# Values in front of seven tables, their rounding some units later, and the output product in front of the low parts

## The reference

```python
def dilated_branch(q, k, v, pos, slopes, window, dil):
    s = einsum(q, keys of the band) * Dh ** -0.5
    s = s - slopes[head] * dist                  # linear in the distance, one slope a head
    s = where(|rel| <= half, s, NEG_INF)
    m = max(s); p = exp(s - m); l = sum(p)
    return (p @ v) / l, m + log(l)

def dilated_attention(q, k, v, pos, slopes):     # (window, dilation): (128, 1), (512, 4), (2048, 16)
    wts = softmax of the three log-denominators
    return sum(wts * the three outputs)

def neighbourhood_attention(q, k, v, rpb):       # a window of 8 rows by 16 columns of a grid, bias from a table
    return softmax(q k^T * d ** -0.5 + bias) @ v
```

## Time and profile before

| what | value |
| --- | --- |
| median of three runs | 4428.1 us |
| the profiled execution's own time | 4431.9 us |
| its span | 4430.1 us |
| TensorE matmul busy | 3857.9 us, 87% |
| VectorE busy | 2207.0 us, 50% |
| ScalarE busy | 1520.0 us, 34% |
| GpSimd busy | 1658.4 us, 37% |
| TensorE in the chain of work that ended last | 69% of the span |
| mean granted TensorE clock | 0.944 |

### The profile page before, as it was taken

The page is one execution under the profiler, slowest core; times in us unless marked ns, Lnnn a source line. Parts: engine busy times, 40 slices in busy tenths (PEclk is TensorE's granted clock), DMA queues, the critical chain, the costliest instruction groups (busy, mean ns, idle before and its releaser), DMA issues.

```text
span 4430.1 us, 53389 instructions
## 1 busy us (share of the span) xinstructions
PE 3857.9 (87%) x19336; PEld 3229.6 (73%) x19336; DVE 2207.0 (50%) x3799; ACT 1520.0 (34%) x2745; POOL 1658.4 (37%) x1380
## 2 busy tenths in 40 slices
PE   2999666788869798996999999689798996999998
PEld 1788555676768587875888888677687875888887
DVE  2444388651266476754454443466576743233333
ACT  2212143652233375652212212233575622222221
POOL 2523023643155361003544444355440015444442
PEclk9999888899979899998999999899899998999999
DMA  7666430733035542221223331135523121111111
GB/s 161 183 187 183 115 94 8 152 93 115 24 103 133 158 110 51 58 82 44 95 86 105 81 105 34 72 98 138 150 62 79 41 81 57 48 49 47 58 39 53
DMA packets 283998, 402.37 MB, mean 91 GB/s; under 512 B 43572, under 2 KB 205492, under 8 KB 283188
## 3 DMA queue, kind: packets, MB, share of 16 engines
q1 hardware_dynamic: 276824, 373.79, 30.3%
q10 hardware_dynamic: 6912, 25.17, 2.0%
HBM read 311.60 MB, written 96.45 MB: 92 GB/s over the span
## 4 chain that ended last, share of the span: by engine, by line
PE 69%; issue 8%; DVE 8%; POOL 5%; DVEq 3%; ACT 3%; SPq 2%; DMA 2%; POOLq 1%; ACTq 0%
PE ps L477 6%; PE ps L479 6%; PE ps L478 6%; PE ps L2218 5%; PE ps L2220 5%; PE ps L2219 5%; PE ps L2234 5%; PE ps L2236 5%; PE ps L2235 5%; PE ps L1720 2%; POOL rs L803 2%; PE ps L1411 2%; PE ps L1412 2%; PE ps L1421 1%; DVEq L1228 1%
## 5 line engine op out<-in xcount | busy, mean ns | idle before, releaser
L426 POOL TENSOR_TENSOR WL<-RAW,WH 128x1024 fp32r<-128x1024 f32 x226 | 556.5, 2476 | 702.1 <-ACT WH L408 691.9
L477 PE MATMUL ps<-WH,XTh 128*128 128x512 f32 (+1 forms) x1536 | 618.9, 403 | 74.3 <-issue 36.6
L479 PE MATMUL ps<-WL,XTh 128*128 128x512 f32 (+1 forms) x1536 | 606.4, 395 | 0.0
L478 PE MATMUL ps<-WH,XTl 128*128 128x512 f32 (+1 forms) x1536 | 605.8, 394 | 0.0
L408 ACT ACTIVATE WH<-RAW 128x1024 fp32r<-128x1024 f32 x226 | 233.6, 1057 | 794.9 <-PE ps L2236 347.4
L2254 DVE TENSOR_TENSOR X<-ps,X 128x512 f32<-128x512 f32 x512 | 349.1, 689 | 253.9 <-PE ps L2236 253.0
L2234 PE MATMUL ps<-WH,Hh 128*128 128x512 f32 x1024 | 401.3, 392 | 4.2 <-DVE X L2254 3.1
L2218 PE MATMUL ps<-XTh,WH 128*128 128x512 f32 x1024 | 400.1, 391 | 1.2 <-issue 1.2
L2219 PE MATMUL ps<-XTl,WH 128*128 128x512 f32 x1024 | 398.8, 389 | 0.0
L2220 PE MATMUL ps<-XTh,WL 128*128 128x512 f32 x1024 | 398.8, 389 | 0.0
L2236 PE MATMUL ps<-WL,Hh 128*128 128x512 f32 x1024 | 398.6, 389 | 0.0
(11 more groups left out here) (260 smaller groups left out, 7949.9 us busy)
## 6 DMA issues: line engine op xcount, KB each, us to landing
RAW<-w_all SPq DMA_DIRECT2D x232, 512.0 KB, 3.7
WM<-w_mod ACTq DMA_DIRECT2D x48, 512.0 KB, 4.3
WM<-w_mod SPq DMA_DIRECT2D x48, 512.0 KB, 3.9
X<-x SPq DMA_DIRECT2D x2, 4096.0 KB, 13.7
X_d<-X SPq DMA_DIRECT2D x2, 4096.0 KB, 13.9
QSd<-QA_d SPq DMA_DIRECT2D x16, 512.0 KB, 3.7
KHd<-KA_d SPq DMA_DIRECT2D x32, 256.0 KB, 5.6
KLd<-KA_d SPq DMA_DIRECT2D x32, 256.0 KB, 6.2
```

The costliest lines, as they stand in the source:

```text
L426: e.tensor_tensor(w_low(n), w_raw(n), w_high(n).bitcast(F32), ALU.subtract).then_inc(w_ready, 1)
L477: e.matmul(bank, a, w, start=(kc == 0), stop=False)
L478: e.matmul(bank, b, w, start=False, stop=False)
L479: j = e.matmul(bank, a, l, start=False, stop=(kc == K - 1))
```

## The change

It is one diff with three parts. SyncE in the dilated stage issues table 0 alone, then V and VFS of the first two heads, then tables 1 to 3, then the load of head 1, then tables 4 to 7. `value_high(0)` on ScalarE moves behind the exponential of unit 2, and `value_low(0)` on GpSimd in front of unit 3's bias (neighbourhood) or unit 2's table update (dilated). And VectorE does the output of a group ahead of the low parts of the same step instead of behind them. The helpers `band_act` and `band_dve` are shared by the neighbourhood and the dilated stage, so the second and third parts are in both; the latent attention has its own.

```diff
--- before.py
+++ after.py
@@ -1509,7 +1509,6 @@
                 e.activation(a.VHL[:, h % 2, :, 0:64], a.VS[:, h // 2 % 2, :, o0:o0 + 64], ACT.Copy)
                 e.drain().then_inc(s["vhi"], 1)
 
-            value_high(0)
             exps(0)
             for u in range(N_UNITS + 6):
                 if 1 <= u <= N_UNITS:
@@ -1518,6 +1517,8 @@
                     exps(u + 1)
                 if u % 4 == 0 and u >= 8:
                     copy_out(u // 4 - 2)
+                if u == 1:
+                    value_high(0)
                 if u % T == 5 and u + 3 < N_UNITS:
                     value_high(u // T + 1)
 
@@ -1582,10 +1583,10 @@
             for u in range(N_UNITS + 10):
                 if u + 1 < N_UNITS:
                     maxes(u + 1)
+                if u % 4 == 1 and u >= 13:
+                    output(u // 4 - 3)
                 if 1 <= u <= N_UNITS:
                     low(u - 1)
-                if u % 4 == 1 and u >= 13:
-                    output(u // 4 - 3)
 
         def value_low(e, a, h):
             s = a.s
@@ -1600,9 +1601,10 @@
 
         def na_pool(who, a):
             e, s = who.e, a.s
-            value_low(e, a, 0)
             for u in range(N_UNITS):
                 h, t = divmod(u, T)
+                if u == 3:
+                    value_low(e, a, 0)
                 if t == 0:
                     e.wait_ge(*a.loaded(h))
                 if u >= 3:
@@ -1630,6 +1631,8 @@
                     e.drain()
                     e.tensor_scalar(LM[:], LM[:], 2.0, None, ALU.mult)
                     e.drain()
+                if u == 2:
+                    value_low(e, a, 0)
                 e.wait_ge(s["max"], a.u0 + u + 1)
                 if g == 0:
                     parts = [(slice(c, 576, 4), slice(128, 272)), (slice(576, DIL_KEYS), slice(272, 384))]
@@ -1679,9 +1682,7 @@
                         e.dma_start(NAB[64 * a2:64 * a2 + 64, slot, :].rearrange("p (a b) -> p a b", b=GRID_W),
                                     NAB_d[h][:, 1 - a2:1 - a2 + NA_E, GRID_W - 1:2 * GRID_W - 1]).then_inc(ld, 16)
                 if a.kind == "dil" and h == 0:
-                    for k in range(3):
-                        for t in range(ND_FIRST[k], ND_FIRST[k + 1]):
-                            e.dma_start(ND[:, t, :], ND_d[t]).then_inc(s[f"nd{k}"], 16)
+                    e.dma_start(ND[:, 0, :], ND_d[0]).then_inc(s["nd0"], 16)
                 if h % 2 == 0:
                     vld = a.v_loaded(p)[0]
                     if p >= 2:
@@ -1695,6 +1696,9 @@
                         if p >= 2:
                             e.wait_ge(s["out"], a.g0 + 4 * p - 4)
                         load_v(e, ZB_d, p, p % 2, ZSn, vld)
+                if a.kind == "dil" and h < 2:
+                    for t in range(ND_FIRST[h + 1], ND_FIRST[h + 2]):
+                        e.dma_start(ND[:, t, :], ND_d[t]).then_inc((s["nd1"], s["nd2"])[h], 16)
 
         def heads_pe(who, a):
             e, s = who.e, a.s
```

## The result

| | kernel before | changed kernel |
| --- | --- | --- |
| median (12 runs each) | 4429.07 us (4424.79 to 4434.16) | 4436.93 us (4433.97 to 4444.76) |
| profiled execution's own time, span | 4431.9, 4430.1 us | 4444.76, 4443.0 us |
| VectorE busy | 2207.0 us | 2211.5 us |

The ratio is 1.0019, interval 1.0010 to 1.0028: slower by some 8 us, where no measurable change had been forecast (4426.8, range 4418 to 4436).

A forecast was written before the change was run, and what follows sets the result against it. TensorE was taken to bound the running dilated stage, but not its start. Dilated starts -4.7, dilated outputs +5.2 and the neighbourhood stage -1.8 gave -1.3 us: 4430.6 profiled, 4426.8 as median, range 4418 to 4436.

The forecast's parts named there:

- The neighbourhood's odd groups: Neighbourhood stage, second group of each pair: Y asks earlier, meets the preceding GpSimd bias piece, scores come sooner; -0.15 a pair.
- rival (b): Neighbourhood stage: Y waits a whole further GpSimd piece, holding low parts and TensorE; +8.4, late tables +3, 4438.2 us; 11%.
- a clock term: Dilated starts: TensorE at half clock after waiting for tables 4 to 7; 1.5 us lost in the first stage, 1.1 second.
- The rows cited against rival (b): Earlier trace: DVE gets in between GpSimd pieces, 2.37 us for one small product beside three pieces without a pause.
- The even groups: Neighbourhood stage, first group of each pair: Y precedes GpSimd's value part, takes 0.42 us; scores -0.58, about 0.4 let through.
- the last group: Neighbourhood stage: the final group's output delays the low part and nothing shortens it; +0.4 us.
- Dilated output ahead of the low parts: Dilated stages, steady part: TensorE waits 0.19 to 0.20 us for the low part at each of 26 outputs; +5.2 us.
- Dilated starts: Both dilated stages: fifth maximum comes earlier though held by tables 4 to 7; -2.5 and -2.2, together -4.7 us.
- The neighbourhood's start: Neighbourhood stage's start: first three biases precede GpSimd's value part, fourth maximum at 798.7 instead of 800.00; -1.3 us.
- N steady: Neighbourhood stage past its start: -0.9 us for six pairs of groups, +0.4 for the final one.

The follow-up runs named there:

- product in PSUM: The changed kernel, with the neighbourhood stage's product with the reciprocals written back to PSUM, so Y has one SBUF input; ratio 1.0003 to the kernel before.
- the first execution: First profiled execution of the changed kernel, no further edit; second dilated stage's start 4.4 us longer than before, -1.7 when run again; ratios 1.0019 and 1.0027.

## Why the prediction was wrong, step by step

- **The neighbourhood's odd groups: the step that failed.** The prediction had Y ask at 893.95, "it meets the piece before, ends at 894.44", -0.15 a pair. Measured, Y took 1.80 us and a pair 1.2 us more, some 7.1 us over six pairs. The 893.95 comes out as about 895.36 less the low parts' 0.81 us (in the kernel before the reciprocal began at 894.61, and the low part, whose place it takes, at 893.80) less the 0.58 us by which the even group was to come earlier.

```profile
893.80 0.69 DVE L1554 TENSOR_TENSOR PTln<-ps,PThn 128x512 fp32r<-128x512 f32 x1
894.61 0.17 DVE L1567 RECIPROCAL li<-rl 128x4 f32<-128x4 f32 x1
```

The prediction moved VectorE by that 0.58 and left GpSimd's pieces where they were, and it put the request 0.17 us ahead of a handover. But the pieces follow the maxima, so they move too: the last piece ahead of Y began 1.3 us after the start of the maximum at 892.85 before, and 1.7 us after the same maximum, at 894.54, in the changed kernel. With VectorE's own 0.81 alone the request is 894.55 in the time of before, inside the last piece, and that is rival (b): Y ends with that piece. So the sum stood on a margin of 0.17 us between two engines whose distance the change itself alters, and the rival that went with the other outcome got 11% and a price of +8.4, where 7.1 was measured.
- **TensorE's clock in the neighbourhood stage: a term put at nothing.** The prediction counted a clock term for the dilated starts and none here. Six falls in the three traces of the changed N code, 1.5 to 1.6 us each, make the steady part +8.7, +10.3 and +11.7 out of +7.1. Each began 2.4 to 4.1 us after an odd Y had asked, at the end of TensorE's wait or behind it, the wait being for that group's low part, and none of the other eleven traces has one in this stretch. That the waits bring the fall on is read from this coincidence; no run isolates it, and 12 of the 18 odd groups had the wait and no fall.
- **The rows cited against rival (b)** were the earlier trace rows, and they were read too kindly. The three pieces of 7.00 us from 1295.71 hand over, by thirds, at 1298.04 and 1300.38; the product asked at 1298.09, 0.05 after a handover, and ended at 1300.46, 0.08 after the next. It did get in between pieces, but only after a whole one: the very loss that the rival described. Both facts, 2.37 us and no pause, stood in the row; the time of the request relative to the handover was not worked out. The other case stood one product ahead in the same timeline:

```profile
1296.49 1.68 DVE L2104 TENSOR_TENSOR RT<-QN,ROC 128x32 f32<-128x32 f32 x1
```

This one asked inside the first piece and ended at 1298.17, 0.13 after the first handover.

- **The even groups** held: Y 0.42 us. With the wait gone from the odd groups too (product in PSUM) the steady part is -1.2, where -0.9 had been forecast for the six pairs and +0.4 for the last group. The -1.2 also has the benefit of an edit that the change does not have.
- **Dilated output ahead of the low parts: right.** +5.2 forecast (0.20 us a group), +5.9 and +6.0 in the traces (0.23), and 0.0 in the run with it undone.
- **Dilated starts: right in mechanism and size, with noise.** Forecast -2.5 and -2.2. Measured with the new loads and late rounding -1.8, -3.8, -1.7, -3.3, -3.8, -1.5 in D1 (mean -2.7) and, without the +4.4 of the first execution, -1.7, -1.6, -0.8, -3.6, -1.8 in D2 (mean -1.9; with it -0.9). The fifth maximum was forecast at 28.3 us after the barrier (1538.5 less 1510.25); it came after 27.2 to 28.1. The clock's part was forecast at 1.5 us. In both stages of these six kernels the clock fell once more behind the fifth maximum, or not at all, and what was given back between the fifth maximum and the 13th goes with it: 1.2 to 1.3 us where it stayed low for 3.4 us (seven starts), 2.7 to 2.8 where for 6.8 us (four), nothing where it did not fall (one). So most of what tells their D1 starts apart is this. In the changed kernel TensorE idled 4.0 us, not the 7.5 of the prediction, and then had a granted clock of 0.51, the 1.2 GHz level:

```profile
1546.00:1550.00 4.00, 3.72 (x16) 3.42 (x17) 2.48 (x6) 2.33 (x8) 1.11 (x3) 0.51 0.00 0
1550.00:1554.00 4.00, 4.00 (x19) 3.58 (x18) 2.80 (x7) 2.96 (x6) 1.42 (x4) 0.63 0.13 34
```

- **What the start step did not ask** is which half of the change brings the gain. It costed loads and rounding together. Apart, the late rounding with the old loads is worth -3.6 to -6.0 in D1 and -6.1 to -7.0 in D2 (four traces, means -5.2 and -6.7), the loads -1.2 and -1.7, and both together -2.7 and -1.9: the load order takes back some 60% of what the rounding gives. It puts the tables that the fifth maximum needs behind all of head 1, and in the changed kernel's two traces that maximum starts 0.12 after the last of them lands.
- **The neighbourhood's start**, forecast -1.3: seven traces with the late rounding there lie between -0.3 and +1.2 (mean +0.2), the seven with the old place, the kernel before among them, between 0.0 and +1.7 (mean +1.0). A gain of about 0.8 us, no more than the scatter.

By these terms, with the means: +11.0 (N steady: 7.1 and the falls of the clock, 3.9) +6.0 (dilated steady) -4.6 (dilated starts) -0.8 gives +11.6, where the ratios say +8.4 and +12.0. The forecast's -1.3 and this differ by 12.9. Of these 11.5 are the N steady part, forecast at -0.5: 7.6 the odd groups with the even ones, 3.9 the clock.

## What to carry to other kernels

When an instruction is moved to where another engine can hold it, work out the moment at which it asks, with both engines moved, and if the answer hangs on a few tenths of a microsecond, count the bad case as likely as the good one, for the whole row of repetitions. What can be held belongs behind the work that others wait for, or should have an operand less in the contested memory. And when a change has several parts, cost each alone: here one part of three gave 13 us, one was worth less than it took from the first, and one cost 17 by the steady parts of the traces (11 to 15 by the ratios). And where an edit makes TensorE wait longer, look at the granted clock of the stretch behind the wait too.

## What the runs showed of the hardware

- The output Y of VectorE, with two SBUF inputs, was never served inside a GpSimd piece in the groups read. It was let in at the handover between two pieces that follow without a pause, where it had asked 0.5 us before (0.80 us, ending 0.28 after the piece), and waited for the next whole piece where it asked a few hundredths after that one began (1.80 us). With one input in PSUM it took 0.42 us beside the same piece. The Trainium skill (SBUF — State Buffer, on the shared port pair) describes the exclusion for a whole instruction; the trace agrees (1.80 us against 0.42, beside pieces 1.53 us apart). The handover, which decided this case, was seen here.
- The product with the reciprocals took the same time written back to PSUM (0.43 us) as written to SBUF (0.42 us), so keeping it in PSUM costs nothing in these groups, and wins 3.2 us over the stage where the output stands behind the low part.
- The clock fell to the 1.2 GHz level for 3.4 us in the middle of a steady stage, behind waits of 2.2 us, and cost 1.5 to 1.6 us each time. Equal code met it one, two or three times, so one trace of such a stage is read to about 3 us only.
